# Column units a stage later, attention's in halves through two buffers of their own, in a chain of two transformer blocks

## The reference

```python
c_act = silu(c)
sh1, sc1, g1, sh2, sc2, g2 = split(c_act @ w_ada[i] + b_ada[i], 6)
u = x * (1 + sc1) + sh1
y = gla_mixer(u) if i == 0 else chunk_attention(u)        # 16 heads in layer 1
x = layer_norm(ALPHA * x + (1 + g1) * y)
u = x * (1 + sc2) + sh2
y = square(relu(u @ w1)) @ w2                              # 1024 -> 4096 -> 1024
x = layer_norm(ALPHA * x + (1 + g2) * y)
```

## Time and profile before

| | |
|---|---|
| median of 3 runs | 972.4 us (972.38 to 973.44) |
| the profiled execution | 973.14 us; its span from the first to the last instruction is 971.4 us |
| granted TensorE clock | 0.998 of full speed, the higher of its two levels |
| TensorE busy | 956.4 us, 98% |
| VectorE busy | 758.1 us, 78% |
| ScalarE, GpSimd busy | 230.6 us, 84.2 us |
| HBM read | 203.42 MB |

### The profile page before, as it was taken

One profiled execution on the slowest core, in us unless ns is written; L12 is line 12 of the kernel. 1 busy time (PEld: TensorE's weight loads), 2 busy tenths in 40 slices (PEclk: granted clock), 3 DMA queues, 4 the chain that ended last, 5 costly groups with the idle time before them and its releaser, 6 DMA issues. The chain is left out here.

```text
span 971.4 us, 14404 instructions
## 1 busy us (share of the span) xinstructions
PE 956.4 (98%) x5386; PEld 712.0 (73%) x5386; DVE 758.1 (78%) x1719; ACT 230.6 (24%) x580; POOL 84.2 (9%) x100
## 2 busy tenths in 40 slices
PE   8999999999999999999999999999999999999996
PEld 4858856858867998757777777689994767777764
DVE  2797687697688898999999888955667877766687
ACT  4134434125433222111000000123333200000002
POOL 2200000100001000000001000056830000000000
PEclk9999999999999999999999999999999999999999
DMA  9955553955555766473679666535444254544511
GB/s 353 370 200 207 214 216 136 362 206 227 191 216 211 293 222 256 176 299 132 260 269 373 267 261 255 200 131 195 153 174 138 107 190 173 217 173 173 174 44 44
DMA packets 31068, 205.38 MB, mean 211 GB/s; under 512 B 3639, under 2 KB 4844, under 8 KB 7708
## 3 DMA queue, kind: packets, MB, share of 16 engines
q1 hardware_dynamic: 27740, 190.94, 52.3%
q0 software_dynamic: 3264, 13.57, 3.7%
HBM read 203.42 MB, written 1.07 MB: 211 GB/s over the span
## 5 line engine op out<-in xcount | busy, mean ns | idle before, releaser
L1983 PE MATMUL bank<-hT,raw 128*128 128x256 f32 x704 | 155.6, 380 | 0.0
L1983 PEld LDWEIGHTS bank<-hT,raw 128*128 128x128 f32 x704 | 132.7, 190 | 20.1 <-issue 2.4
L983 DVE CUSTOM_DVE_ANT_0 raw<-raw,crow 128x1024 f32<-128x1024 f32 x96 | 113.2, 1222 | 11.0 <-DMA raw<-units_dram 9.4
L2343 PE MATMUL bank<-yT,arena 128*128 128x512 f32 x224 | 100.8, 593 | 0.1
L2343 PE MATMUL bank<-raw,arena 128*128 128x512 f32 x180 | 86.8, 593 | 0.0
L2343 PEld LDWEIGHTS bank<-yT,arena 128*128 128x128 f32 x224 | 42.3, 190 | 53.1 <-issue 50.9
L2371 PEld LDWEIGHTS bank<-hT,raw 128*128 128x128 f32 x416 | 50.4, 192 | 11.5 <-issue 11.5
L840 ACT ACTIVATE arena<-bank 128x512 f32<-128x512 f32 x26 | 15.6, 598 | 179.3 <-PE bank L2371 179.3
L2371 PE MATMUL bank<-hT,raw 128*128 128x128 f32 x416 | 50.6, 275 | 0.0
L1025 DVE SCALAR_TENSOR_TENSOR arena<-arena 128x256 f32<-128x256 f32 x120 | 49.2, 485 | 0.1
L2371 PE MATMUL bank<-arena,gateT 128*128 128x128 f32 x336 | 42.2, 275 | 1.2 <-issue 1.2
(11 more groups left out here) (473 smaller groups left out, 1782.0 us busy)
## 6 DMA issues: line engine op xcount, KB each, us to landing
raw<-units_dram SPq DMA_DIRECT2D x178, 1024.0 KB, 4.9
arena<-ln_rows_dram POOLq DMA_DIRECT2D x4, 1024.0 KB, 6.0
arena<-gate_scratch POOLq DMA_DIRECT2D x4, 512.0 KB, 6.8
arena<-att_line_dram POOLq DMA_DIRECT2D x4, 512.0 KB, 4.9
arena<-small_dram POOLq DMA_DIRECT2D x2, 896.0 KB, 11.2
raw<-units_dram SPq DMA_DIRECT2D x2, 704.0 KB, 8.3
xt<-x_dram SPq DMA_DIRECT2D x2, 512.0 KB, 5.8
arena<-post_g_dram POOLq DMA_DIRECT2D x2, 512.0 KB, 8.8
```

Of the source, the lines that this page charges most:

```text
L983: ins = dve.tensor_tensor_reduce(out=w, in0=w, in1=crow[:], scale=1.0, scalar=0.0, op0=ALU.mult, op1=ALU.add, accum_out=dst[:, c:c + 1])
L1983: mm = pe.matmul(b[:, c * S:(c + 1) * S], raw[:, s, k * 256 + c * P:k * 256 + (c + 1) * P], act_t[:, k, :], start=(k == 0), stop=(k == KC ...
L2343: mm = pe.matmul(SB[i][:], x, y, start=g == 0, stop=stop)
```

## The change

The 48 column units keep their number and their instruction. Their places change:

- Layers 0 and 1 of the first block have six each instead of twelve (`A1 = 6`), the gated linear attention eleven and the first feed-forward 13, as before. Of these 13, the one of group 1 moves to the end of the group, each one after it moves a group later up to g = 7, where two stand ("duaa"); from g = 8 they stand as before.
- Eight units are done in attention as 16 halves of 128 x 1024, through `half_unit` on VectorE. They come from a tensor of their own, `ada_att`, into two buffers in turn (`ada`, which was a scratch buffer, and a new `wlast`). ScalarE issues these loads, `load_half(i)`, of 512 KB each; load i waits until half i - 2 is done.
- The second feed-forward has four, in its groups 1 to 4.
- `coefficients(0)` to `(3)` follow the new order: (2) in group 8 of the first feed-forward instead of group 12, (3) in attention behind half 15 instead of group 12.

In `groups`, `up_sums(up[3])` goes to where the column unit of group 1 was. In layers 0 and 1 the banks A[1] and A[3] swap roles in the output products, and the first of them waits for the last maxima (`nm_ready`) instead of a copy. At the end the first tile is stored in two halves, and VectorE's steps of the two tiles are interleaved. GpSimd stores and loads each gate row later than before; several semaphores are merged, so ScalarE's and VectorE's first waits for `pre` now also await the load of `rel_bias`.

```diff
-A1 = 12
+A2 = 12
+A1 = 6
 U1 = W1 + A1
 T1 = U1 // SLOTS
...
+ORDER = "wwwawwa" "wwwawwa" "wwawwa" "wwww"
 W_AT = [n for n, c in enumerate(ORDER) if c == "w"]
...
-FF_ORDER = ("u" + 2 * "ud" + "aua" + 11 * "dua" + "ddud", "u" + 14 * "ud" + "dud")
+FF_ORDER = ("u" + 2 * "ud" + "ua" + 5 * "dua" + "duaa" + 5 * "dua" + "ddud", 
+            "u" + 2 * "ud" + "ua" + 3 * "dua" + 8 * "du" + "ddud")
 N_GLA = DEPTH * U1
 N_FF0 = N_GLA + len(GLA_ORDER)
...
         HB = ((G[2], G[3]), (A[2], A[3]))
-        UB = ((A[3], A[0]), (A[1], A[2]))
+        UB = ((A[1], A[0]), (A[3], A[2]))
...
-        early = sb("early", [P, 4, P])
+        early, wlast = sb("early", [P, 4, P]), sb("wlast", [P, D])
+        att_half = (ada, wlast)
         EARLY_BANKS = {1: G[3], 3: G[1]}
...
         LAST_BANKS = (A[0], A[2], A[1], A[3])
-        OUT_PARTS = ((0, slice(0, D)), (1, slice(0, 512)), (1, slice(512, D)))
+        OUT_PARTS = [(t, slice(512 * h, 512 * (h + 1))) for t in range(NT) for h in range(2)]
         bc_ready, cur_ready = event("bc_ready", 1), event("cur_ready", 2)
...
-        OUT_W.append([[ada[:], xs[:, 1, :], row(tline), crow[:]],
+        OUT_W.append([[ada[:], xs[:, 1, :], row(tline), wlast[:]],
                       [at_end[:, 0:D], flat_tsum[:, 0:D], at_end[:, D:2 * D], flat_tsum[:, D:2 * D]]])
...
-        OUT_BANKS = DEPTH * [(A[3], G[0], G[1], A[1], A[2], A[0], G[2])] + [(A[0], G[0], G[2], G[1], A[1], A[3], A[2]),
+        OUT_BANKS = DEPTH * [(A[1], G[0], G[1], A[3], A[2], A[0], G[2])] + [(A[0], G[0], G[2], G[1], A[1], A[3], A[2]),
                                                                         (G[0], G[1], A[0], G[3], A[1], G[2], A[2])]
         OUT_BLOCKS = ((0, 0), (0, 1), (1, 1), (1, 0))
...
             x_square(0, 0)
-            act.wait_ge(pre_in, 16 * DEPTH)
+            act.wait_ge(pre_in, 16 * (DEPTH + 1))
             layer_input(0, 0, 0, KC)
             act.wait_ge(x_in[1], 16)
...
@@ -925,20 +934,36 @@
                 h0 = HE + H * qd
                 head_exp(h0, 0)
                 head_exp(h0, 1)
+                if 0 < qd < H - 1:
+                    load_half(5 * qd + 1)
+                    load_half(5 * qd + 2)
                 head_scaled(h0, 0)
                 head_scaled(h0, 1)
                 head_copy(h0, 0, (A[3], A[0]), True)
                 head_copy(h0, 1, (A[3], A[0]), True)
                 head_exp(h0, 2)
                 head_exp(h0, 3)
+                if more:
+                    load_half(5 * qd + 3)
                 head_scaled(h0, 2)
                 head_scaled(h0, 3)
                 head_copy(h0, 2, (A[3], A[0]), True)
                 head_copy(h0, 3, (A[3], A[0]), True)
                 if more:
+                    load_half(5 * qd + 4)
                     keys(qd + 1)
-
+                    load_half(5 * qd + 5)
+
+            def load_half(i):
+
+                if i >= 2:
+                    act.wait_ge(half_used, i - 1)
+                act.dma_start(att_half[i % 2][:], ada_att[i // 2, :, i % 2 * D:(i % 2 + 1) * D]).then_inc(half_in[i % 2], 16)
+
+            for i in range(2):
+                load_half(i)
             keys(0)
+            load_half(2)
             for qd in range(H - 1):
...
-                        gate_columns(l, n)
+            def ada_unit(i):
+
+                n, g, j = ADA_AT[i], i // A2, i % A2
+                if j < 2 * H:
+                    column_unit(n, acc[:, g // 2, 16 * (g % 2) + 2 * j:16 * (g % 2) + 2 * j + 2])
                 else:
-                    column_unit(n, acc[:, 0, 16 * l + 2 * (a - 4):16 * l + 2 * (a - 4) + 2])
+                    column_unit(n, gacc[:, g, 2 * (j - 2 * H):2 * (j - 2 * H) + 2])
+                if j == A2 - 1:
+                    wait_used(dve, 0, n)
+                    dve.wait_ge(gla_in, 48)
+                    dve.scalar_tensor_tensor(gcol[:, g, :], gacc[:, g, :], 1.0, colb[:, B_GATE + KC * g:B_GATE + KC * (g + 1)],
+                                             ALU.add, ALU.add).then_inc(gcol_ready, 1)
+
+            def half_unit(i):
+
+                w = att_half[i % 2][:]
+                dve.wait_ge(half_in[i % 2], 16 * (i // 2 + 1))
+                ch.pass_waits()
+                dve.tensor_tensor_reduce(out=w, in0=w, in1=crow[:], scale=1.0, scalar=0.0, op0=ALU.mult, op1=ALU.add,
+                                         accum_out=acc[:, 1, 16 + i:17 + i]).then_inc(half_used, 1)
             def silu_row():
...
-                wait_used(dve, 0, (A_AT[A1 - 1], U1 + A_AT[A1 - 1], ADA_1[19], ADA_1[19])[s])
-                dve.wait_ge(colb_ready, 16)
+                if s == 3:
+                    dve.wait_ge(half_used, 2 * (AF1 - AH))
+                else:
+                    wait_used(dve, 0, ADA_AT[A2 * s + 2 * H - 1])
+                dve.wait_ge(gla_in, 48)
                 dve.tensor_tensor(shsc[:, c], acc[:, lay, c], colb[:, B_ADA + 32 * lay + 16 * i:B_ADA + 32 * lay + 16 * (i + 1)],
...
                     coefficients(0)
-                ada_unit(l, 10)
                 s0, s1, s2, s3 = OUT_S
-                out_sum(l, 1, s0, A[3][:], None)
+                out_sum(l, 1, s0, A[1][:], None)
                 out_told(l, 2, 0, s0, G[0][:])
                 y_block(l, 0)
                 out_sum(l, 3, s1, s0, A[0][:])
...
                                       ALU.add, ALU.mult).then_inc(sum_ready, 1)
...
-                    o = slice(t, t + 1)
+                    for h in range(2):
+                        c = slice(h * 512, (h + 1) * 512)
+                        ch.do(dve.scalar_tensor_tensor(xs[:, t, c], xt[:, t, c], nmean[:, t:t + 1], ln_row[:, 0, c],
+                                                       ALU.add, ALU.mult))
+
+                def deviation(t):
+
                     dve.wait_ge(dev_ready, t + 1)
-                    ch.do(dve.tensor_scalar(neg[:, o], ssx[:, o], -0.5 / D, -0.5 * LN_EPS, ALU.mult, ALU.add))
+                    ch.do(dve.tensor_scalar(neg[:, t:t + 1], ssx[:, t:t + 1], -0.5 / D, -0.5 * LN_EPS, ALU.mult, ALU.add))
                     inv_root_of(3, t)
-                    for u, c in OUT_PARTS:
-                        if u == t:
-                            dve.scalar_tensor_tensor(xt[:, t, c], xs[:, t, c], rst[:, o], ln_row[:, 1, c], ALU.mult,
-                                                     ALU.add).then_inc(xu_ready.sem, 1)
+
+                def finished(t, h):
+
+                    c = slice(h * 512, (h + 1) * 512)
+                    dve.scalar_tensor_tensor(xt[:, t, c], xs[:, t, c], rst[:, t:t + 1], ln_row[:, 1, c], ALU.mult,
+                                             ALU.add).then_inc(xu_ready.sem, 1)
                 dve.wait_ge(lnrow_in, 16 * 4)
-                residual_sum(0)
+                residual_half(0, 0)
+                residual_half(0, 1)
+                mean(0)
                 scaled(0)
-                finished(0)
-                residual_sum(1)
+                residual_half(1, 0)
+                deviation(0)
+                finished(0, 0)
+                residual_half(1, 1)
+                mean(1)
+                finished(0, 1)
                 scaled(1)
-                finished(1)
+                deviation(1)
+                finished(1, 0)
+                finished(1, 1)
...
-                if lay == 0 and AG + g < len(ADA_1):
-                    ada_unit_1(ADA_1[AG + g], AG + g)
-                    if AG + g == len(ADA_1) - 1:
+                if (AF0, AF1)[lay] + g < (AH, 4 * A2)[lay]:
+                    ada_unit((AF0, AF1)[lay] + g)
+                    if AF0 + g == 2 * A2 + 2 * H - 1 and lay == 0:
                         coefficients(2)
-                        coefficients(3)
             def groups(s):
...
@@ -1702,21 +1725,23 @@
                             dve.tensor_tensor(w, w, gate_row[:, GATE_ROW[1, 1], :], ALU.mult).then_inc(w_gated, 1)
                     up_half_sums(s, g + 1)
                     if g == 1:
-                        side_unit(lay, 0)
+                        up_sums(up[3], 3)
                     else:
                         weight_sums(down[g])
                     up_rest_sums(s, g + 1)
                     hidden_sums(s, g + 1, (g + 1) % 3)
-                    if g < SEVEN - 2:
+                    if 1 != g < SEVEN - 2:
                         up_sums(up[g + 2], g + 2)
-                    else:
+                    elif g > 1:
                         weight_sums(down[SEVEN - 1], wsum_last)
                     if g == 0:
                         wait_used(dve, 0, down[0])
                         weight_sums(down[1])
                     if 1 <= g <= 4:
                         x_piece(s - 1, g - 1)
-                    if g > 0:
+                    if 0 < g < 8:
+                        side_unit(lay, g - 1)
+                    if g >= 7:
                         side_unit(lay, g)
                 dve.wait_ge(row_in[s], 16)
...
             stage_tiles(2)
             token_sums(2, tsum, quad_tsum)
+            half_unit(0)
...
```

(22 more changed lines are left out.)

149 lines of the change are left out of this document (58 added, 91 removed).

## The result

The changed kernel takes 997.8 us (median of four, 996.6 to 1001.4) against 972.4 us before: ratio 1.0261, 95% interval 1.0248 to 1.0274. Slower, as forecast, but by 25.4 us where 10.8 were forecast, and outside the range; 25.4 is also more than the forecast's terms give with every high end taken (some 20). The profiled execution took 998.0 us (span 996.2), so it is 24.9 above the profiled one of before.

The account below looks back on a forecast made before the run. TensorE's own work bounds the kernel (busy 98%). Attention +11.6, fourth group -1.2, double unit +0.8, coefficients -0.3, end -0.1 sum to +10.8 on the median 972.4: 983 predicted, range 975.5 to 989.5.

Parts of the forecast that it names:

- the fourth groups: Feed-forwards: `up_sums(3)` comes earlier, so TensorE's waits of 0.58 and 0.65 us for it go: -1.2 (0 to -1.5).
- the double unit: First feed-forward, g = 7: two column units in one group make VectorE late for the next weight sums: +0.8 (0 to 1.8).
- the coefficients: First feed-forward, group 13: two coefficient blocks of the last column unit, which made it late, go elsewhere: -0.3 us.
- Rival (c): Attention: VectorE's idle 7.9 us per quad absorbs five halves' 6.1; 971.6 us, or 969.8 with low ends; chance 0.15.
- Rival (a): Attention: halves' loads land before VectorE asks, so only the work counts: 5.8 us less, 977.4; chance 0.17.
- the passages: Attention, from one quad to the next: halves delay the next quad's maxima, 3.0, 3.0 and 5.6 us, +11.6 in all.
- I take 3.6: Attention: a half's 512 KB load lands after 3.6 us, between a store's 2.7 and a 1024 KB load's 4.6.
- x pieces 3.1: Attention: VectorE's two x pieces behind the halves take 3.1 us, between 2 x 1.22 alone and 3.82 beside GpSimd.
- My sum holds none of it for them: Attention: halves also suffer the VectorE–GpSimd SBUF lock by the skill's rule, but the sum adds 0 for it.
- rival (b): Attention: the lock decides; some seven halves beside GpSimd's sums stretch by 0.7 us each, value rows stay slow: 990; chance 0.12.
- The issues between exponentials and scaling: Attention, quads 1 and 2: ScalarE issues two loads between exponentials and scaling, 0.35 us each, 0.7 a passage.
- Column units a stage later: 0: Whole kernel: column units a stage later, reordered ring and merged semaphores cost 0; weights come no later.

Follow-up runs that it names:

- the spread kernel: The changed kernel with all 16 halves kept but placed where VectorE is idle, loads moved with their buffers, `coefficients(3)` in quad 3: 981.9 us, ratio 1.0099.
- the four kernels above: The changed kernel (997.8 us), and it with 2 of 16 loads (990.4), with GpSimd's sums on 8 of 128 columns (994.4), with both (976.7).

## Why the prediction was right and wrong

**Right.** TensorE's own work bounds the kernel; attention has no slack between the maxima and the transposes, so each microsecond at the maxima was one of TensorE (7.0 and 7.0, and 10.1 of 10.4); the halves `5qd+1` and `5qd+2` cost nothing (the distance stays at 1.55 from 661 to 688); the fourth groups (-1.2 forecast, -1.56 measured), the double unit (+0.8, +0.70), the coefficients (-0.3, -0.28), the end (-0.1, -0.2), and the wait that moved from the bank to SiLU (0 and 0) hold. Rival (c) is out: the halves were not absorbed. Rival (a) had 977.4 for loads that are never waited for; that kernel took 990.4, and 976.7 only with GpSimd's sums small as well.

**Wrong, the passages: 3.0 + 3.0 + 5.6 = 11.6 forecast, 24.4 measured.** Three steps of the sum failed.

- "I take 3.6" for a landing is right for a load with none issued shortly ahead of it (3.5 to 4.1) and was the wrong question: at the moment of issue SyncE's and GpSimd's loads go out too, and it is 7.3, 7.0 and 9.0. Whether a load is alone could have been read off the trace before: there SyncE issues 1 MB at 674.38, 1.1 us ahead of the 675.45 from which the sum counts. This was the dearest: in the first passage 3.4 of the 4.7 us by which the maxima came later than the sum had them, in the third 3.2 of 4.4, and there one half more stood behind the landing than in the sum (1.2). The 3.2 that the forecast worked out beside its 3.6 lies below every landing traced.
- "x pieces 3.1" was 4.49, above the high end of 3.82, as they met a later part of GpSimd's sums.
- "My sum holds none of it for them": a half beside those sums took 3.62. In the first passage of the changed kernel the landing hides this; as soon as the loads come in time, the stretch costs 13.7 by the medians and 9.7 by the maxima. The rule of the Trainium skill (SBUF — State Buffer, Who interferes with whom) was cited and then left to rival (b), whose price of 0.7 a half was too low as well: 2.4 for one half here, and 4.4 in the spread kernel.

Taken away together, landing and stretch leave 3.7 us of loss. TensorE's clock stood nowhere in the sum; in the changed kernel that cost little. The issues between exponentials and scaling, 0.7 in the sum, cost nothing: the fourth of the transposes starts 3.97 us behind the maxima and did so 3.96 behind them before.

**Wrong, the zeros.** "Column units a stage later: 0" left out two moved steps. `coefficients(1)` went from the start of the GLA stage into a full stretch of it, and VectorE was 0.65 late at a norm that it had finished at 430.04 before, with TensorE ready for it at 430.13; the steps of its four instructions take 0.66 (392.03 to 392.69; first and last):

```profile
392.03 0.17 DVE L1098 TENSOR_TENSOR arena<-acc,colb 128x16 f32<-128x16 f32 x1
...
392.52 0.17 DVE L1112 TENSOR_TENSOR arena<-nt,arena 128x8 f32<-128x8 f32 x1
```

And GpSimd's copies of a bias block came at 527.8, 10 us later than before, as GpSimd now stores and loads a gate row ahead of their load. They fell beside VectorE's sums of up weights in group 6 (timelines of GpSimd, VectorE and TensorE):

```profile
528.36 1.50 POOL L604 COPY arena<-arena 128x1024 f32<-128x1024 f32 x1
...
528.99 1.41 DVE L1620 TENSOR_TENSOR arena<-raw,arena 128x512 f32<-128x512 f32 x1
...
530.51 1.69 PE L2406 MATMUL bank<-arena 128*128 128x128 f32 x13 [0.65 <-issue]
```

1.41 for a sum of 128 x 512 that takes 0.69 elsewhere, and TensorE is 0.81 late. Two kernels with the same feed-forward bear this out. With three halves a quad VectorE's sum begins first, at 527.96, with the copy at 528.13: it takes 0.77 and the wait is missing. With the products of zeros added the copy begins first, at 527.82, with the sum at 528.46: it takes 1.42 and the wait is there. No run moved the four instructions of `coefficients(1)` alone; that wait is read off the rows.

**Not resolved.** How 24.4 divides between landing and stretch has no one answer, as they overlap and as the clock takes its own share; the four kernels above are the answer. That the third landing is 9.0 because of GpSimd's 1 MB load at 734.65 and SyncE's at 737.67 is argued from the times; no run took these away.

## What to carry to other kernels

Before work goes into an engine's idle time, ask what runs beside it there: which other engine reads SBUF, which loads leave in the same microsecond. Two causes can each hide the other, so an experiment that removes one shows too little; remove both, and then each. And a wait of TensorE can cost more than its length, as its clock can fall behind it; an experiment that shortens one wait can so move the loss in place of removing it.

## What was not expected of the hardware

- A two-input instruction of VectorE, 1.22 us alone, took 3.62 and 5.62 us beside back-to-back sums of GpSimd: in the spread kernel it began at 675.15 and ended at 680.77, and GpSimd went through three whole sums meanwhile, so it waited for more than one of them.
- The granted clock of TensorE was 0.50 for some 6 us behind an idle of 2.74 us; kept busy with products of zeros, it stayed at 1.00. By the Trainium skill (TensorE: Matmul & The Clock Gate, The HAM clock gate) an idle TensorE's clock is halved; the trace agrees. The length of the idle alone doesn't decide it. With GpSimd's sums small TensorE idles 2.94 us twice, at full clock behind the first and at half behind the second (timeline, then windows):

```profile
693.78 1.24 PE L2046 MATMUL bank<-kst,probs 128*128 128x128 f32 x6 [2.94 <-ACT probs L653]
...
723.03 1.59 PE L2046 MATMUL bank<-kst,probs 128*128 128x128 f32 x6 [2.94 <-ACT probs L653]
```

```profile
694.00:696.00 2.00, 1.86 (x16) 1.12 (x16) 0.93 (x4) 1.34 (x4) 0.00 (x0) 1.00 0.98 365
724.00:726.00 2.00, 2.00 (x11) 1.15 (x10) 0.17 (x1) 0.65 (x2) 0.00 (x0) 0.50 0.97 391
```

- In the changed kernel the fallen clock costs little, since TensorE would have waited for the probabilities anyway: of 1.86 us of slow records at 756.40 to 760 only some 0.3 are lost, the third passage being 10.4 long where its maxima slipped by 10.1.
- A load of 512 KB landed in 3.5 to 4.1 us where no load had been issued in the 4 us ahead of it (six of the 16 in the changed kernel; the very first took 5.8, of which its issue took 2.1), and in 7.0, 7.3 and 9.0 us where one of SyncE's stood 0.5 us ahead and one of GpSimd's 0.5 to 3.6 us; 10.1 for the third of these in the kernel with one column unit a group.
